# A mixture-of-experts loop on one core: the next block's gather, the bias products and the turning of the gates change their places among the weight pieces

## The reference, cut to what matters

```
gu = xb @ w_gu[e] + b_gu[e]              # 1024 -> 2048, float32
gate, up = split(gu)
gate = min(gate, 7); up = clip(up, -7, 7)
act = (up + 1) * gate * sigmoid(1.702 * gate)
out = act @ w_down[e] + b_down[e]        # 1024 -> 1024
y   = sum over the 4 experts of a token of gates * out
```

## Time and profile before

| | us |
|---|---|
| median of three runs (1522.66 to 1524.72) | 1522.77 |
| profiled execution, its own time | 1524.9 |
| its span, first to last instruction | 1523.1 |
| PE matmuls busy | 1461.6 (96%) |
| DVE / ACT / POOL busy | 519.6 / 263.8 / 114.1 |
| first matmul of the expert loop | 599.77 |

### The profile page before, as it was taken

How to read it: one execution, slowest core, us unless ns; L and a number is a source line. 1 busy time by engine, 2 the same in 40 slices (tenths; PEclk the granted TensorE clock), 3 DMA queues, 4 the chain that set the end, 5 groups by cost and what they waited for, 6 DMA issues and landing times.

```text
span 1523.1 us, 23088 instructions
## 1 busy us (share of the span) xinstructions
PE 1461.6 (96%) x9245; PEld 743.2 (49%) x9245; DVE 519.6 (34%) x980; ACT 263.8 (17%) x604; POOL 114.1 (7%) x100
## 2 busy tenths in 40 slices
PE   9999999999999998999999999999999999999896
PEld 7777776556777764333333333333333333333332
DVE  3652788767410156122122212211212112122123
ACT  1224214631210014100101001001001001100102
POOL 1002241010503402000000000000000000000000
PEclk9999999999999999999999999999999999999998
DMA  6346687556269648999999999999999999999995
GB/s 211 111 168 179 209 271 232 175 167 195 89 216 331 247 164 316 428 426 429 426 427 428 429 427 429 429 428 428 428 430 428 428 428 429 430 427 428 429 429 205
DMA packets 110621, 507.80 MB, mean 333 GB/s; under 512 B 12600, under 2 KB 49056, under 8 KB 85888
## 3 DMA queue, kind: packets, MB, share of 16 engines
q1 hardware_dynamic: 103884, 499.63, 82.0%
q10 hardware_dynamic: 6676, 7.29, 1.6%
HBM read 491.18 MB, written 15.72 MB: 333 GB/s over the span
## 4 chain that ended last, share of the span: by engine, by line
PE 61%; DMA 25%; DVE 3%; ACT 1%; issue 1%; DVEq 0%; SPq 0%; ACTq 0%
DMA wGU<-in_w_gu 24%; PE ps L2394 12%; PE ps L2399 11%; PE ps L1898 10%; PE ps L2381 5%; PE ps L2202 3%; PE ps L1912 3%; PE ps L2308 2%; PE ps L2216 2%; PE ps L2229 2%; PE ps L2342 2%; PE ps L2316 1%; DMA ringS<-in_ssd_proj 1%; ACT xs L1267 1%; PE ps L2329 1%
## 5 line engine op out<-in xcount | busy, mean ns | idle before, releaser
L2394 PE MATMUL ps<-wGU,xe 128*64 128x512 f32 x1536 | 342.4, 594 | 18.5 <-DMA wGU<-in_w_gu 17.8
L2399 PE MATMUL ps<-wD,aT 128*64 128x512 f32 x1024 | 226.8, 595 | 0.0
L2394 PEld LDWEIGHTS ps<-wGU,xe 128*64 128x64 f32 x1536 | 107.8, 137 | 234.5 <-issue 197.8
L1898 PE MATMUL ps<-xT,ring 128*128 128x288 f32 (+1 forms) x864 | 179.8, 409 | 1.2 <-PEq L200 0.7
L1898 PEld LDWEIGHTS ps<-xT,ring 128*128 128x128 f32 (+1 forms) x864 | 125.1, 170 | 46.0 <-issue 3.5
L2399 PEld LDWEIGHTS ps<-wD,aT 128*64 128x64 f32 x1024 | 70.7, 137 | 131.8 <-issue 127.9
L2381 PE MATMUL ps<-wGU,xe 128*64 128x512 f32 x512 | 121.3, 594 | 11.9 <-DMA wGU<-in_w_gu 11.9
L1791 DVE TENSOR_SCALAR sg<-sg 128x512 f32<-128x512 f32 x32 | 13.7, 427 | 335.4 <-ACT sg L1262 335.4
L1798 DVE COPY ysb<-ps 64x512 f32<-64x512 f32 x32 | 22.2, 694 | 304.8 <-PE ps L2403 304.8
L1262 ACT ACTIVATE sg<-ps 128x512 f32<-128x512 f32 x32 | 19.1, 598 | 471.1 <-PE ps L2386 471.1
L402 PE MATMUL ps<-xT,ring 128*128 128x288 f32 x320 | 78.1, 407 | 0.0
(11 more groups left out here) (476 smaller groups left out, 1445.1 us busy)
## 6 DMA issues: line engine op xcount, KB each, us to landing
wGU<-in_w_gu SPq DMA_DIRECT2D x128, 2048.0 KB, 37.0
wD<-in_w_down SPq DMA_DIRECT2D x64, 2048.0 KB, 37.0
ring<-in_w_in SPq DMA_DIRECT2D x21, 2048.0 KB, 9.2
out<-hst SPq DMA_DIRECT2D x8, 1024.0 KB, 6.0
ringS<-in_ssd_proj SPq DMA_DIRECT2D x4, 2048.0 KB, 10.1
wbuf<-prompt_A_rows ACTq DMA_DIRECT2D x16, 384.0 KB, 4.0
out<-Sb SPq DMA_DIRECT2D x2, 2048.0 KB
ring<-in_hg_proj SPq DMA_DIRECT2D x2, 2048.0 KB, 7.8
```

Of the source, the lines that this page charges most:

```text
L1898: last = m.matmul(ps[h, b, 0:T], ring[c % 2][:, k, n * P + h.start:n * P + h.stop], xT[:, k, :], start=(k == 0), stop=(k == KD - 1))
L2394: last = m.matmul(ps[half[h], bank, :], xe[:, f, hx, :], wgu[n][:, k, col + CW * h:col + CW * h + CW], start=(i == 0 and k == 0), stop=False)
L2399: last = m.matmul(ps[half[h], B_Y, :], aT[:, k, i - 4, :], wdn[n][:, k, CW * h:CW * h + CW], start=(i == 4 and k == 0), stop=False)
```

## The change

On PE the gather for the next block moves from behind piece 3 to ahead of piece 2. All four bias products move from inside piece 3 to ahead of it, so that piece 3 ends both halves with weight matmuls. `turn_g` stays ahead of `turn_a`, but now follows piece 3 at once. The wait of the gather on `xs` goes; an earlier wait of the same engine covers it. The gate half now raises `m_u` once a block; DVE waits for the up half on the fourth `m_f` of the block. No instruction that computes is added or removed.

```diff
 ACT
-                    act.wait_ge(m_u, b * 2 + 1)
+                    act.wait_ge(m_u, b + 1)
                     a.activation(sg[:], ps[:, B_G, :], ACT.Sigmoid, scale=SALPHA).then_inc(m_sg, 1)
 DVE
-                    dve.wait_ge(m_u, b * 2 + 2)
+                    dve.wait_ge(m_f, b * 6 + 4)
                     dstep(v.tensor_scalar(up[:], ps[:, B_U, :], LIMIT + 1.0, 1.0 - LIMIT, ALU.min, ALU.max))
 PE
-                        if i == 4:
+                        if i == 2:
                             pe.wait_ge(m_p, b + 2)
-                            pe.wait_ge(m_xs, b + 1)
                             for t in (2, 0, 1):
                                 gather(t)
+                        if i == 3:
+                            pe.wait_ge(m_g, b * 2 + 2)
+                            for bank, col in ((B_G, 0), (B_U, D)):
+                                for h in range(2):
+                                    m.matmul(ps[half[h], bank, :], esel[:], bg3[:, col + CW * h:col + CW * h + CW], start=False, stop=False)
+                        if i == 4:
                             if pair is not None:
                                 pe.wait_ge(m_sa, pair * NSC + NSC)
                             turn_g()
...
                         pe.wait_ge(m_w[n], loaded)
                         if i == 3:
-                            pe.wait_ge(m_g, b * 2 + 2)
                             for bank, col in ((B_G, 0), (B_U, D)):
                                 for k in range(2):
                                     for h in range(2):
                                         last = m.matmul(ps[half[h], bank, :], xe[:, 2 + k, 1, :],
-                                                        wgu[n][:, k, col + CW * h:col + CW * h + CW], start=False, stop=False)
-                                if bank == B_U:
-                                    last.then_inc(m_f, 1)
-                                for h in range(2):
-                                    last = m.matmul(ps[half[h], bank, :], esel[:], bg3[:, col + CW * h:col + CW * h + CW], start=False, stop=True)
-                                last.then_inc(m_u, 1)
+                                                        wgu[n][:, k, col + CW * h:col + CW * h + CW], start=False, stop=(k == 1))
+                                last.then_inc(m_u if bank == B_G else m_f, 1)
                             continue
```

## The result

The changed kernel takes 1530.70 us, the median of ten runs (1529.51 to 1534.72); the kernel before took 1524.05 us in ten runs beside it. The ratio is 1.0043, 95% interval 1.0029 to 1.0057. So it is **slower by 0.43%**, some 6.6 us, and lies above the predicted range.

A forecast was written before the change was run, and what follows sets the result against it. DMA was taken to set the end, PE only early in the loop. Transfers lose 1.6 us, 1.1 us is saved behind the last ones: +0.5 us, median 1522.77 to 1523.3 us, range 1521.3 to 1526.5.

The forecast's parts named there:

- Piece 3 to piece 4: From piece 3's start to piece 4's in a block: 6.66 us in place of 7.75, 1.09 us shorter.
- The cost of a block: Early in the loop, gather and bias products no longer hidden: 1.93 - 1.09 = 0.84 us more per block on PE.
- The size of the stock: Loaded pieces ahead of PE at the loop's start: 24.8 us, gone near block 13 before, near block 25 after.
- Block 0: PE waits for the selection matrix `psel` ahead of the moved gather, losing 1.4 us once.
- The transfers: Slots come free later early in the loop, so transfers lose 1.6 us, with ends 0 and 3.4.
- Behind the last transfers: In the last block PE reaches pieces 4 and 5 earlier, both already landed: 1.09 us saved once.
- Does the stock last to the end?: Over the loop: no, used up near block 25, then DMA sets the end; 7.5 us in hand, 0.24 a block.
- The clock falls: PE's clock at 1.2 GHz after the new hole, pieces 4 and 5 taking 14 us; about 200 us more; chance 0.02.
- PE becomes the bound to the end: Hole ahead of `turn_a` in all blocks: past 6.98 us from piece 3 to 4, over 0.2% slower; chance 0.14.

The follow-up runs named there:

- e5: Changed kernel plus five full-width bfloat16 matmuls, their output unused, behind the turned gates; 1.0015 of the kernel before.
- e1: Changed kernel with the gather back behind piece 3, bias products still ahead of piece 3; 0.9998 of the kernel before.
- e10: Changed kernel with six of the gather's 14 matmuls behind the turned gates, in block 0 the whole gather there; 0.9993 of the kernel before.
- e6: Changed kernel with the gather's last six matmuls behind the turned gates, the other eight ahead of piece 2; 1.0006 of the kernel before.
- e7: Changed kernel with the whole gather behind the turned gates, none ahead of piece 2; 0.9995 of the kernel before.
- e4: Changed kernel with the gather of block 0 alone left behind piece 3; 1.0039 of the kernel before.
- e9: Changed kernel with every gather matmul cut to 128 of its 512 columns, as many instructions; 1.0002 of the kernel before.
- e3: Changed kernel plus five pairs of matmuls, their output unused, behind the turned gates; 1.0093 of the kernel before.
- e8: Changed kernel with the gather picking one of three bfloat16 parts of each prompt token, six of 14 matmuls left; 1.0164 of the kernel before.

## Why the prediction was wrong, point by point

- **Piece 3 to piece 4: right.** 6.66 forecast, 6.64 in block 0 (621.50 - 614.86), which stands ahead of the loop, 6.75 in the loop. The 0.09 more stand ahead of DVE's clip of `up`: inside the loop its new wait is worked out from the loop's counter, 0.05 us on DVE's sequencer and 0.05 to start.
- **The cost of a block: right in kind, a little small.** Half of 56.6 - 54.73 is 0.94 us, with 0.84 forecast. Of the 0.24 a block in hand this took 0.10.
- **The size of the stock: a little small.** 24.8 us, used up near block 13 before and near block 25 after the change, was reckoned; the first wait for a piece comes in block 15 before and in block 27 in e5. What is in hand at the end was counted from the last block and doesn't hang on it.
- **Block 0: right.** 1.3 us forecast as 1.4.
- **The transfers: a term of the sum, mis-sized.** 1.6 us was taken; e5 shows 2.4 (894.4 - 892.0), inside the stated ends 0 to 3.4, where one execution stands against one (3.9 against e1, which would lie outside). The pieces for blocks 3 and 4 took 9.3, 10.2 and 9.4 us from issue to landing, with 8.7 taken. With 2.4 the sum would have been +1.3, and e5 has 0.0015 x 1523 = 2.3 (0.9 to 3.7 by its interval).
- **Behind the last transfers: nearly right,** 0.9 us in e10 with 1.09 forecast, but only where transfers still set the end.
- **"Does the stock last to the end?" and the rival "The clock falls": here it failed.** The sum took PE's clock as 1.00 in every block, so the falls stood in it at nothing. In hand at the end were 7.5 us by the forecast; the block's 0.10 takes 3 of them. What was really there is the distance to e5, which has the same blocks without the falls. Piece 4 of the last block starts 1506.06 - 601.03 = 905.0 us after the loop's first matmul in the changed kernel, without the falls it would be 905.0 - 8.4 = 896.6, and in e5, where PE waits for transfers, it is 1501.84 - 600.59 = 901.2. So 4.6 us were in hand, and the falls cost 8.4: PE ends 3.8 us behind the transfers. These are 1.4 us late themselves, since it was 1499.60 - 599.77 = 899.8 before. That makes the 5.2 us by which the loop is longer; the other 1.3 of the 6.5 us between the spans lie ahead of the loop, with the fall at 130 us. So it was the rival "PE becomes the bound to the end", by another door than the one named there: not a longer chain, but the clock. The clock had been priced as all or nothing, in every block and for both pieces, 200 us, and given 0.02. It falls in some blocks and costs 1.68 us each, which is enough because only 4.6 us were in hand.
- **The row that misled:** the window with PE busy for 0.68 of 2 us at a clock of 1.00 has weight matmuls on both sides of the wait. The new stretch has 3.2 us of transposes and idle time; the one before has 697.78 - 695.51 = 2.3 us, and behind it the clock never fell. The Trainium skill, "TensorE: Matmul & The Clock Gate", section "Part 4: PE-mode transpose", says that transposes don't count as work for the clock as matmuls do. The falls agree with it: every one in the changed kernel stands behind such a stretch. By that section the place at issue was the whole stretch, not the hole in it; no run here tells the two apart, since filling the hole (e5, e6, e7, e10) shortens what is free of other matmuls as well.

## What to carry to other kernels

An engine that starts with a stock of loaded data pays for every instruction until the stock is used up, so a move into waits that only exist later has to be held against the stock, and the margin that is left should be larger than what a rival thought unlikely would cost: here a few falls of 1.68 us against 4.6. Before a stretch of transposes and waiting is laid open on PE, put matmuls that have to be done anyway into it: the gather behind the turned gates (e7) keeps the clock at no cost that the timing can tell. A fall of the clock is worth repairing only where PE is the bound.

## What the runs showed of the hardware that was not expected

- The clock falls in some blocks only, though all blocks run the same instructions with the same hole: 5 of 32 in the change, 7 in e4, 6 in e9, and in other blocks each time. It isn't mere scatter: the steps between the blocks are 7, 3, 7 and 3 in the change (10, 17, 20, 27, 30), and in e4 they are 7 and 3 in turn from block 4 on (2, 4, 11, 14, 21, 24, 31). What makes this pattern stays open.
- Lists of another length made PE stand at the turns of the loop: some 2 us a turn with 20 more matmuls and weight loads in a block (e3), some 6.5 us in two waits with 16 fewer (e8), none with 10 more (e5), none in the change and in e9, which has as many instructions. Neither more nor fewer is the rule; where the loop's code comes to lie may be, but that was not tried.
